# The MLP's up projection: two of its three products per chunk put side by side in one product of 512 columns

## The chip, the cores and the metric

The kernel runs on one core of a Trainium2 chip. The metric is device time in microseconds (us), the median of three runs. A core has TensorE (matrix products into the accumulator memory, PSUM), VectorE, ScalarE, GpSimd and SyncE, each with its own queue of instructions that it works off in order. They wait for each other by semaphores only.

## The reference, cut to what matters

Two transformer blocks follow each other on 256 tokens with 1024 features. The change lies in the MLP of the second block, a squared-ReLU MLP with 4096 hidden features, in float32:

```
h2 = rmsnorm(x, norm_mlp_g[l])
x = x + jnp.square(jax.nn.relu(h2 @ w_mlp_up[l])) @ w_mlp_down[l]
```

## The kernel before, in words

Float32 accuracy comes from products of a shorter type (fp32r). A number is split into a high part and a low part, and `W*X` becomes three products: high weights by high rows, high weights by low rows, low weights by high rows. `WH` and `WL` hold the two parts of the weights, in four buffers (`NB`) of 128x1024 each; one such buffer is a "unit". `XH` and `XL` hold the two parts of the rows, `HH` and `HL` those of the hidden features, both of the latter in two buffers.

The MLP is 64 units in groups of four: two up units (`k % 4` is 0 or 1) and two down units (2 or 3), so there are 16 groups. In the texts below they are called up 0, up 1, down 0 and down 1 of a group.

- An up unit (function `up` of TensorE) makes 128 hidden features of all 256 tokens. It runs over eight chunks of 128 input features, with three products of 256 columns each (`triple`, lines 1819 to 1821), all summed in the first 256 columns of bank 0 (up 0) or bank 1 (up 1). The weights are the stationary operand, the rows stream.
- VectorE then takes the ReLU out of the bank (line 1769) and squares it (line 1771), ScalarE rounds the square to its high part (line 1055), and VectorE subtracts that to have the low part (line 1774, `HL`).
- A down unit (`token_unit`, lines 2025 to 2027) multiplies the hidden features with 1024 columns of weights: 12 products of 512 columns, in which the weights stream. It waits for `relu_low`, the semaphore of line 1774: down 0 for the features of up 0, down 1 for those of up 1.

Beside that each unit has to be split: ScalarE copies it to its high part (`high2`, line 638, released by `unit_used`, which TensorE gives at the end of a unit, so that a buffer is free), and VectorE subtracts it from the weights (`low2`, line 1113, released by `unit_high`). TensorE waits for it by `unit_split`.

The order of the work is the order of the code. For a step k VectorE does `low2` of the unit three steps ahead, and then, if k is an up unit, the ReLU, the square and the low part of k's features. ScalarE does `high2` of the unit three steps ahead and then the high part of k's features. So on VectorE the ReLU of up 1 stands behind the split of the next group's up 0, and on ScalarE that split stands behind the rounding of up 0's features.

Of the kernel before, what the change touches and what calls it, by code (L numbers as in the profile page):

```python
# [8 lines left out]
F32R = mybir.dt.float32r  # L9
BF16 = mybir.dt.bfloat16  # L10
I32 = mybir.dt.int32
ALU = mybir.AluOpType
# [4 lines left out]
P = 128  # L17
D = 1024
DC = D // P
S = 256  # L20
META = 16
T = S + META
# [97 lines left out]
def build(nc, A, out):  # L120

    ctx = ExitStack()
    with ctx:
        def sb(name, shape, dt=F32):
            return ctx.enter_context(nc.sbuf_tensor(name, shape, dt))
# [5 lines left out]
        def const(name):  # L131
# [6 lines left out]
            scalar=("meta_std", "router_high", "mix_std", "group_exp", "pair_exp", "lambda_exp"),  # L138
# [18 lines left out]
        def ev(name):  # L157

            if name not in made:
                made[name] = ctx.enter_context(nc.semaphore(name))  # L160
            return made[name]
# [4 lines left out]
        big = sb("big", [P, ARENA + 8448])  # L166
        WH = sb("WH", [P, NB, UNIT], F32R)
        WL = sb("WL", [P, NB, UNIT], F32R)
        XH = sb("XH", [P, DC * T], F32R)
        XL = sb("XL", [P, DC * T], F32R)  # L170
        HH = sb("HH", [P, 2, S], F32R)
        HL = sb("HL", [P, 2, S], F32R)
        hT = sb("hT", [P, DC, T])
# [29 lines left out]
        ps = ctx.enter_context(nc.psum_tensor("ps", [P, 8, 512], F32))  # L203
# [55 lines left out]
        def z(g):  # L259
            return big[:, Z0 + g * SLAB:Z0 + (g + 1) * SLAB].rearrange("p (c t) -> p c t", c=DC)  # L260

        zx, zg, zq, zk, _, _, zc, zi = (z(g) for g in range(8))
# [33 lines left out]
        X8 = lambda t, n: t[:, 0:DC * n].rearrange("p (c t) -> p c t", c=DC)  # L296
        xh1, xl1 = X8(XH, T), X8(XL, T)
        xh2, xl2 = X8(XH, S), X8(XL, S)
        sel_part = lambda k: sel_flat[:, k * S:(k + 1) * S]
        mix_hi = [sel_part(0), sel_part(1), xh2[:, 6, :], xh2[:, 7, :], HH[:, 0, :], HH[:, 1, :], xh2[:, 2, :], xh2[:, 3, :]]  # L300
        mix_lo = [sel_part(2), sel_part(3), xl2[:, 6, :], xl2[:, 7, :], HL[:, 0, :], HL[:, 1, :], xl2[:, 2, :], xl2[:, 3, :]]
# [787 lines left out]
        def _(dve):  # L1089
            v = nc.vector  # L1090
# [16 lines left out]
            def low2(k):  # L1107
                if k >= U2:
                    return
                dve.wait_ge(ev("unit_high"), U1 + k + 1)  # L1110
                src, h = pack2(k, WH[:, k % NB, :])
                _, dst = pack2(k, WL[:, k % NB, :])
                v.tensor_tensor(dst, src, h.bitcast(F32), ALU.subtract).then_inc(ev("unit_split"), 1)  # L1113
# [62 lines left out]
            for c in range(DC):  # L1176
                dve.wait_ge(ev("x_high"), c + 1)
                v.scalar_tensor_tensor(out=xl1[:, c, :], in0=ps[:, c, 0:T], scalar=g1("pre_mix_norm", c),
                                       in1=xh1[:, c, :].bitcast(F32), op0=ALU.mult, op1=ALU.subtract)\
# [159 lines left out]
            for t in range(TT):  # L1339
# [4 lines left out]
                                       op0=ALU.mult, op1=ALU.add).then_inc(ev("mixed"), 1)  # L1344
# [5 lines left out]
                                       op0=ALU.mult, op1=ALU.add).then_inc(ev("h_mixed"), 1)  # L1350
# [4 lines left out]
            for c in range(DC):  # L1355
                dve.wait_ge(ev("turned_high"), c + 1)
                v.scalar_tensor_tensor(out=xl2[:, c, :], in0=of_chunk(c), scalar=g1("pre_ffn_norm", c),
                                       in1=xh2[:, c, :].bitcast(F32), op0=ALU.mult, op1=ALU.subtract)\
# [14 lines left out]
            for t in range(TT):  # L1373
                chain(v.scalar_tensor_tensor(out=logit[:, t, :], in0=ps[:, 3 * t, 0:nr], scalar=st(5, t),
                                             in1=b_router[:], op0=ALU.mult, op1=ALU.add))
            for t in range(TT):
                chain(v.scalar_tensor_tensor(out=logit[:, t, :], in0=ps[:, 3 * t, nr:2 * nr], scalar=st(5, t),
                                             in1=logit[:, t, :], op0=ALU.mult, op1=ALU.add))
# [19 lines left out]
            for t in range(TT):  # L1398
# [11 lines left out]
                                         op0=ALU.add, op1=ALU.mult))  # L1410
# [86 lines left out]
            for t in range(TT):  # L1497
                dve.wait_ge(ev("sh_gate"), t + 1)
                v.scalar_tensor_tensor(out=sact[:, t, :], in0=ps[:, (3, 0)[t], 0:FF], scalar=st(5, t), in1=sact[:, t, :],
                                       op0=ALU.mult, op1=ALU.mult).then_inc(ev("sh_hidden"), 1)  # L1500
# [48 lines left out]
            with dve.If(more > 0):  # L1549
                with dve.Fori(0, ROUNDS - 1) as r:  # L1550
# [4 lines left out]
                    with dve.Fori(0, QUADS) as q:  # L1555
                        b = r * QUADS + q
# [22 lines left out]
            for t in range(TT):  # L1579
# [3 lines left out]
                                             in0=ps[:, 4 + 2 * t:6 + 2 * t, :], scalar=st(8, t),  # L1583
                                             in1=gain_ffn.rearrange("p (b n) -> p b n", b=2),
                                             op0=ALU.mult, op1=ALU.mult))
                v.scalar_tensor_tensor(out=in_order(ffn_tmp[:, t, :]), in0=by_row(h_tok[:, t, :]), scalar=st(4, t),
                                       in1=in_order(ffn_tmp[:, t, :]), op0=ALU.mult, op1=ALU.add)\
# [6 lines left out]
            for c in range(DC):  # L1594
                dve.wait_ge(ev("turned_high"), DC + c + 1)
                v.scalar_tensor_tensor(out=xl2[:, c, :], in0=of_chunk(c), scalar=g2("norm_mix_g_2", c),
                                       in1=xh2[:, c, :].bitcast(F32), op0=ALU.mult, op1=ALU.subtract)\
# [11 lines left out]
            for k in range(48):  # L1609
# [4 lines left out]
                if 8 <= k < 16:  # L1614
                    c = k - 8
                    dve.wait_ge(ev("unit_taken_by_scalar"), TAKEN_S1 + c + 1)
                    w = lambda tap: g2("conv_w_2", 8 * tap + c)
                    chain(v.tensor_scalar(zc[:, c, :], zx[:, c, :], w(3), g2("conv_b_2", c), ALU.mult, ALU.add))
                    for back in (1, 2, 3):
                        ins = v.scalar_tensor_tensor(out=zc[:, c, back:], in0=zx[:, c, 0:S - back],  # L1620
                                                     scalar=w(3 - back), in1=zc[:, c, back:], op0=ALU.mult,
                                                     op1=ALU.add)
# [10 lines left out]
                if 30 <= k < 34:  # L1633
# [5 lines left out]
                                           op1=ALU.mult).then_inc(ev("one_plus_a"), 1)  # L1639
# [5 lines left out]
                if 39 <= k < 43:  # L1645
                    if k == 39:
                        dve.wait_ge(ev("lru_input"), 4)
                    for c in (2 * (k - 39), 2 * (k - 39) + 1):
                        v.tensor_tensor_scan(out=zc[:, c, :], data0=zx[:, c, :], data1=zi[:, c, :], initial=0.0,
                                             op0=ALU.mult, op1=ALU.add).then_inc(ev("scanned"), 1)  # L1650
# [15 lines left out]
            for n in range(HEADS2):  # L1666
                j, qt = divmod(n, TT)
                keys = (qt + 1) * P
                b = n % 2
# [5 lines left out]
                for h in range(2):  # L1675
                    ins = v.tensor_tensor_scan(out=cum(b)[:, h, S - keys:S][:, ::-1], data0=omb[:, h, ::-1],  # L1676
                                               data1=ones[:, 0:1].to_broadcast([P, keys]), initial=1.0,
                                               op0=ALU.mult, op1=ALU.mult)
# [83 lines left out]
            for k in range(64):  # L1762
                if k < 63:
                    low2(U_MLP + 3 + k)
                if k % 4 < 2:
                    f = (k // 4) * 2 + k % 4
                    dve.wait_ge(ev("unit_used"), U1 + U_MLP + k + 1)
                    x_ = ps[:, k % 4, 0:S]
                    v.tensor_scalar(zx[:, 2 + f % 2, :], x_, 0.0, None, ALU.max).then_inc(ev("relu"), 1)
                    dve.wait_ge(ev("relu"), f + 1)  # L1770
                    v.tensor_tensor(zx[:, f % 2, :], zx[:, 2 + f % 2, :], zx[:, 2 + f % 2, :], ALU.mult)\  # L1771
                        .then_inc(ev("relu_done"), 1)
                    dve.wait_ge(ev("relu_high"), f + 1)
                    v.tensor_tensor(HL[:, f % 2, :], zx[:, f % 2, :], HH[:, f % 2, :].bitcast(F32), ALU.subtract)\  # L1774
                        .then_inc(ev("relu_low"), 1)
                if k == 10:
                    dve.wait_ge(ev("tok_square"), 5 * TT)
                    chain(v.tensor_scalar(st(12), st(12), 1.0 / D, EPS, ALU.mult, ALU.add))
                    chain(v.reciprocal(st(13), st(12)))
# [24 lines left out]
            for t in range(TT):  # L1804
# [3 lines left out]
                                       op0=ALU.mult, op1=ALU.mult).then_inc(ev("out_tokens"), 1)  # L1808
# [5 lines left out]
        def _(pe):  # L1814
            mm = nc.tensor.matmul

            def triple(o, h, l, rh, rl, first, last, skip=False):

                mm(o, h, rh, start=first, stop=False, skip_group_check=skip)  # L1819
                mm(o, h, rl, start=False, stop=False, skip_group_check=skip)  # L1820
                return mm(o, l, rh, start=False, stop=last, skip_group_check=skip)  # L1821
# [101 lines left out]
            b = uk % NB  # L1923
            for h in range(HEADS):
                if h >= 4:
                    pe.wait_ge(ev("nope_keys_taken"), h - 3)
                w = slice(h * NOPE, h * NOPE + P)
# [6 lines left out]
            for k in range(3):  # L1934
                w = slice(HEADS * NOPE, UNIT)
# [83 lines left out]
            def used_after(last):  # L2019
                last.then_inc(ev("unit_used"), 1)  # L2020
# [8 lines left out]
            for k in range(4):  # L2029
                pe.wait_ge(ev("mix_low"), in_mix(k))  # L2030
                for t in range(TT):
                    last = mix_rows(k, t, 4)
# [8 lines left out]
            for k in range(4, 8):  # L2041
                last = mix_rows(k, 0, 0)
# [29 lines left out]
            for c in range(DC):  # L2072
# [5 lines left out]
                for t in range(TT):  # L2078
# [3 lines left out]
                    last = mm(ps[:, 3 * t, 0:nr], xl2[:, c, tk], router_hi[:, c, :], start=False, stop=c == DC - 1,  # L2082
                              skip_group_check=True)
# [112 lines left out]
            for f in range(2):  # L2196
                for t in range(TT):
                    last = tr(ps[:, 2, f * S + t * P:f * S + (t + 1) * P], sact[:, t, f * P:(f + 1) * P], ident[:])
# [16 lines left out]
            for k in range(2):  # L2215
                un = u0 + 4 + k
                pe.wait_ge(ev("unit_split"), un + 1)
                for t in range(TT):
                    tk = slice(t * P, (t + 1) * P)
                    for n in range(2):  # L2220
                        last = triple_rows(ps[:, 4 + 2 * t + n, :], HH[:, k, tk], HL[:, k, tk], un % NB, n, k == 0, False,
                                           skip=True)
# [44 lines left out]
            with pe.If(more > 0):  # L2267
                pe.wait_ge(ev("ffn_summed"), TT)
                pe.sem_inc(ev("o_by_tensor"), 1)
                with pe.Fori(0, ROUNDS - 1) as r:  # L2270
                    with pe.Fori(0, QUADS) as q:
                        b = r * QUADS + q
# [4 lines left out]
                        for t in range(TT):  # L2277
                            last = tr(ps[:, 3, t * P:(t + 1) * P], sel_w[:, t, 0:SLOTS], ident[:])
# [102 lines left out]
            for n in range(HEADS2):  # L2381
# [9 lines left out]
                for h in range(2):  # L2391
                    for k in range(nk):
                        last = tr(ps[:, (4, 7)[n % 2], (h * nk + k) * P:(h * nk + k + 1) * P],
                                  att(n % 2)[:, h, k * P:(k + 1) * P], ident[:])
# [6 lines left out]
            for c in range(2):  # L2401
                for t in range(TT):
                    last = tr(ps[:, c, t * P:(t + 1) * P], p_tok(t)[:, c * P:(c + 1) * P], ident[:])
# [27 lines left out]
            for c in range(4, DC):  # L2431
                pe.wait_ge(ev("split_low"), SP_AT["y_att"] + c + 1)
                last = token_unit(U_BRA + c, c, 0, xh2, xl2, 4, False, c == DC - 1)
# [16 lines left out]
            for c in range(4, DC):  # L2450
                last = token_unit(U_OUT + c, c, 0, xh2, xl2, 0, False, c == DC - 1)
# [13 lines left out]
            def up(k, arrived=False):  # L2465

                pe.wait_ge(ev("unit_split"), U1 + U_MLP + k + 1)
                b = (U_MLP + k) % NB
                for c in range(DC):
                    if arrived:  # L2470
                        pe.wait_ge(ev("rows_low"), 4 + 2 + c // 4 + 1)
                    w = slice(c * P, (c + 1) * P)
                    last = triple(ps[:, k % 4, 0:S], WH[:, b, w], WL[:, b, w], xh2[:, c, :], xl2[:, c, :], c == 0,
                                  c == DC - 1)
                used_after(last)

            for k in range(62):
                if k % 4 < 2:
                    up(k, k == 0)
                else:  # L2480
                    f = (k // 4) * 2 + k % 2
# [5 lines left out]
            for f in range(2):  # L2487
                pe.wait_ge(ev("relu_low"), 30 + f + 1)
                last = token_unit(U_MLP + 62 + f, f, 0, HH, HL, 4, False, f == 1)
# [14 lines left out]
            for c in range(4, DC):  # L2504
                pe.wait_ge(ev("rows_low"), 10)
                last = token_unit(U_PLE + c, c, 0, xh2, xl2, 4, False, c == DC - 1)
# [21 lines left out]
```

## Time and profile before

| | |
|---|---|
| median of three runs | 913.47 us (910.93 to 914.49) |
| the profiled execution's own time | 910.93 us |
| its span in the trace | 909.1 us |
| TensorE products, busy | 811.3 us (89%) |
| VectorE busy | 490.1 us (54%) |
| ScalarE busy | 380.0 us (42%) |
| mean TensorE clock granted | 0.956 |

The trace gives each instruction its start and its length. Ends of products are modelled, since they overlap; their starts are what counts, and the distance from one start to the next is called the pitch here. In an answer by groups, "idle before" is the time in which the engine stood still just ahead of these instructions, with the engine and line that released it. Weight loads are listed apart (PEld), since they overlap with products. The granted clock is a share of 2.4 GHz. The MLP takes the stretch from 691.6 us to some 872 us of the span.

### The profile page before, as it was taken

The page shows a single profiled execution, that of the slowest core. Times are in us where ns is not written, and L with a number is a line of the kernel's source. Part 1 is how long each engine was busy: PE and PEld are TensorE (multiplying, and loading weights), DVE is VectorE, ACT ScalarE, POOL GpSimd, SP SyncE. Part 2 cuts the span into 40 slices and gives each one's busy share as a digit, 9 for nine tenths or more (in the row PEclk, how much of TensorE's full clock was granted, in tenths as well). Part 3 has the DMA queues.
Part 4 walks back from the last instruction along what each step waited for, and adds up shares of the span by engine and source line. Part 5 has one row for each costly group of instructions (what it writes and reads, how often), then busy time and mean ns, then how long its engine had stood idle before and what let it go on. Part 6 is the DMA issues. An engine that isn't in the chain of part 4 may idle for free.

```text
span 909.1 us, 13427 instructions
## 1 busy us (share of the span) xinstructions
PE 811.3 (89%) x5498; PEld 646.6 (71%) x5498; DVE 490.1 (54%) x813; ACT 380.0 (42%) x633; POOL 48.3 (5%) x114
## 2 busy tenths in 40 slices
PE   6988999997786676779999998799999999999995
PEld 5967878764343333449989885477787999999974
DVE  6786648411110030064926687855677666666665
ACT  5563567310000100065456845535445544444454
POOL 5000030101010001000000000000000000000000
PEclk9998999999897989899999997999999999999998
DMA  8951154699999999996428552065454555555101
GB/s 278 376 188 47 48 217 177 251 411 423 422 420 420 421 421 421 413 345 212 139 70 306 193 197 81 1 240 177 161 186 144 187 187 190 189 189 195 65 1 46
DMA packets 75949, 205.80 MB, mean 226 GB/s; under 512 B 5720, under 2 KB 48896, under 8 KB 63600
## 3 DMA queue, kind: packets, MB, share of 16 engines
q1 hardware_dynamic: 67406, 150.44, 46.3%
q0 software_dynamic: 8480, 54.49, 14.9%
q8 instruction: 45, 0.74, 0.3%
q14 instruction: 16, 0.13, 0.0%
q10 hardware_dynamic: 2, 0.00, 0.0%
HBM read 203.87 MB, written 1.05 MB: 225 GB/s over the span
## 4 chain that ended last, share of the span: by engine, by line
PE 67%; DMA 16%; DVE 10%; ACT 4%; issue 2%; SPq 0%; POOL 0%; ACTq 0%; DVEq 0%
DMA big<-in_w_up 13%; PE ps L2025 10%; PE ps L2026 10%; PE ps L2027 10%; PE ps L1819 8%; PE ps L1821 7%; PE ps L1820 7%; PE ps L2138 4%; DMA big<-in_w_down 3%; PE ps L2119 1%; DVE big L1676 1%; PE ps L2152 1%; DVE WL L1105 1%; DVE WL L1113 1%; ACT WH L638 1%
## 5 line engine op out<-in xcount | busy, mean ns | idle before, releaser
L1113 DVE TENSOR_TENSOR WL<-big,WH 128x1024 fp32r<-128x1024 f32 x154 | 186.8, 1224 | 117.6 <-ACT WH L638 116.7
L638 ACT ACTIVATE WH<-big 128x1024 fp32r<-128x1024 f32 x154 | 160.6, 1054 | 83.0 <-PE ps L2027 82.5
L1819 PE MATMUL ps<-XH,WH 128*128 128x256 f32 (+1 forms) x640 | 187.4, 293 | 1.7 <-DVE WL L1105 0.7
L1820 PE MATMUL ps<-XL,WH 128*128 128x256 f32 (+1 forms) x640 | 183.1, 286 | 0.0
L1821 PE MATMUL ps<-XH,WL 128*128 128x256 f32 (+1 forms) x640 | 183.0, 286 | 0.0
L1819 PEld LDWEIGHTS ps<-XH,WH 128*128 128x128 f32 x640 | 123.6, 193 | 7.3 <-issue 4.4
L1820 PEld LDWEIGHTS ps<-XL,WH 128*128 128x128 f32 x640 | 123.8, 193 | 0.8
L1821 PEld LDWEIGHTS ps<-XH,WL 128*128 128x128 f32 x640 | 123.5, 193 | 0.0
L2138 PE MATMUL ps<-big 128*32 128x256 f32 x1024 | 75.7, 461 | 44.1 <-DMA big<-in_w_gate 26.4
L2138 PEld LDWEIGHTS ps<-big 128*32 128x32 f32 x1024 | 42.3, 132 | 78.7 <-issue 67.7
L2025 PE MATMUL ps<-WH,XH 128*128 128x512 f32 x240 | 94.4, 393 | 2.9 <-issue 1.1
L2027 PE MATMUL ps<-WL,XH 128*128 128x512 f32 x240 | 93.5, 390 | 0.0
L2026 PE MATMUL ps<-WH,XL 128*128 128x512 f32 x240 | 93.5, 389 | 0.0
L1481 DVE TENSOR_TENSOR big<-big,ps 128x256 f32<-128x256 f32 x8 | 3.4, 422 | 124.9 <-ACT big L873 124.8
L2025 PE MATMUL ps<-WH,HH 128*128 128x512 f32 x152 | 59.9, 394 | 0.6 <-DVE HL L1774 0.6
L2026 PE MATMUL ps<-WH,HL 128*128 128x512 f32 x152 | 59.4, 391 | 0.0
L2027 PE MATMUL ps<-WL,HH 128*128 128x512 f32 x152 | 59.2, 390 | 0.0
L2025 PEld LDWEIGHTS ps<-WH,XH 128*128 128x128 f32 x240 | 45.1, 188 | 13.6 <-issue 1.5
L1105 DVE TENSOR_TENSOR WL<-big,WH 128x1024 fp32r<-128x1024 f32 (+1 forms) x39 | 40.4, 1045 | 26.1 <-ACT WH L629 25.9
L2027 PEld LDWEIGHTS ps<-WL,XH 128*128 128x128 f32 x240 | 45.1, 188 | 9.6
L2026 PEld LDWEIGHTS ps<-WH,XL 128*128 128x128 f32 x240 | 45.1, 188 | 9.0
L1055 ACT ACTIVATE HH<-big 128x256 fp32r<-128x256 f32 x32 | 13.4, 418 | 76.1 <-DVE big L1771 76.1
(396 smaller groups left out, 1096.6 us busy)
## 6 DMA issues: line engine op xcount, KB each, us to landing
big<-in_w_in SPq DMA_DIRECT2D x35, 1024.0 KB, 9.5
big<-in_w_gate SPq DMA_DIRECT2D x16, 1024.0 KB, 15.6
big<-in_w_up SPq DMA_DIRECT2D x16, 1024.0 KB, 15.7
big<-in_w_gate POOLq DMA_DIRECT2D x16, 1024.0 KB, 18.8
big<-in_w_up POOLq DMA_DIRECT2D x16, 1024.0 KB, 19.4
big<-in_w_down SPq DMA_DIRECT2D x16, 1024.0 KB, 16.1
big<-in_w_down POOLq DMA_DIRECT2D x16, 1024.0 KB, 19.4
big<-in_w_mlp_up SPq DMA_DIRECT2D x16, 1024.0 KB, 5.5
```

Of the source, the lines that this page charges most:

```text
L638: s.activation(dst, src, ACT.Copy).then_inc(ev("unit_high"), 1)
L1055: s.activation(HH[:, f % 2, :], zx[:, f % 2, :], ACT.Copy).then_inc(ev("relu_high"), 1)
L1105: v.tensor_tensor(dst, src, h.bitcast(F32), ALU.subtract).then_inc(ev("unit_split"), 1)
L1113: v.tensor_tensor(dst, src, h.bitcast(F32), ALU.subtract).then_inc(ev("unit_split"), 1)
L1676: ins = v.tensor_tensor_scan(out=cum(b)[:, h, S - keys:S][:, ::-1], data0=omb[:, h, ::-1], data1=ones[:, 0:1].to_broadcast([P, keys]), ini ...
L1819: mm(o, h, rh, start=first, stop=False, skip_group_check=skip)
L1820: mm(o, h, rl, start=False, stop=False, skip_group_check=skip)
L1821: return mm(o, l, rh, start=False, stop=last, skip_group_check=skip)
L2025: mm(o, h, WH[:, b, w], start=first, stop=False, skip_group_check=skip)
L2026: mm(o, l, WH[:, b, w], start=False, stop=False, skip_group_check=skip)
L2027: return mm(o, h, WL[:, b, w], start=False, stop=last, skip_group_check=skip)
L2138: last = mm(ps[j * CAP:(j + 1) * CAP, 1, up * FF:(up + 1) * FF], x(c)[:, j * CAP:(j + 1) * CAP], slot(first_slot + j)[:, c * FF:(c + 1) * FF],
```

## The change

The high and low parts of the rows become two planes of one tensor, `XHL`, so that one product can read 256 columns of each. Per chunk, `up` now issues one product of 512 columns (high weights by high rows and by low rows, into the two halves of a bank) and one of 256 columns (low weights by high rows, into the first half). The bank's halves are then to be added: VectorE copies the first half out, adds the second, and takes ReLU and square in one instruction. The rest of the kernel is as it was, but for line numbers (1113 becomes 1114, 1774 becomes 1777, 2025 to 2027 become 2028 to 2030).

```diff
-        XH = sb("XH", [P, DC * T], F32R)
-        XL = sb("XL", [P, DC * T], F32R)
+        XHL = sb("XHL", [P, 2, DC * T], F32R)
+        XH, XL = XHL[:, 0], XHL[:, 1]
...
+        both2 = lambda c: XHL[:, :, c * S:(c + 1) * S]
...
                     dve.wait_ge(ev("unit_used"), U1 + U_MLP + k + 1)
-                    x_ = ps[:, k % 4, 0:S]
-                    v.tensor_scalar(zx[:, 2 + f % 2, :], x_, 0.0, None, ALU.max).then_inc(ev("relu"), 1)
+                    chain(v.tensor_copy(zx[:, 2 + f % 2, :], ps[:, k % 4, 0:S]))
+                    v.tensor_tensor(zx[:, 2 + f % 2, :], zx[:, 2 + f % 2, :], ps[:, k % 4, S:2 * S], ALU.add)\
+                        .then_inc(ev("relu"), 1)
                     dve.wait_ge(ev("relu"), f + 1)
-                    v.tensor_tensor(zx[:, f % 2, :], zx[:, 2 + f % 2, :], zx[:, 2 + f % 2, :], ALU.mult)\
+                    v.scalar_tensor_tensor(out=zx[:, f % 2, :], in0=zx[:, 2 + f % 2, :], scalar=0.0,
+                                           in1=zx[:, 2 + f % 2, :], op0=ALU.max, op1=ALU.mult)\
                         .then_inc(ev("relu_done"), 1)
...
-                    last = triple(ps[:, k % 4, 0:S], WH[:, b, w], WL[:, b, w], xh2[:, c, :], xl2[:, c, :], c == 0,
-                                  c == DC - 1)
+                    mm(ps[:, k % 4, :].rearrange("p (h n) -> p h n", h=2), WH[:, b, w], both2(c), start=c == 0, stop=False)
+                    last = mm(ps[:, k % 4, 0:S], WL[:, b, w], xh2[:, c, :], start=False, stop=c == DC - 1)
```

On VectorE, a stretch of the MLP before, from the low part of up 1's features on (L1113 is `low2`; `HL` the low part of the hidden features):

```order
L1774 TENSOR_TENSOR HL<-big,HH 128x256 [waits relu_high]
L1113 TENSOR_TENSOR WL<-big,WH 128x1024 [waits unit_high] x3
L1769 TENSOR_SCALAR big<-ps 128x256 [waits unit_used]
L1771 TENSOR_TENSOR big<-big 128x256 [waits relu]
L1774 TENSOR_TENSOR HL<-big,HH 128x256 [waits relu_high]
L1113 TENSOR_TENSOR WL<-big,WH 128x1024 [waits unit_high]
L1769 TENSOR_SCALAR big<-ps 128x256 [waits unit_used]
L1771 TENSOR_TENSOR big<-big 128x256 [waits relu]
L1774 TENSOR_TENSOR HL<-big,HH 128x256 [waits relu_high]
```

And the same stretch now:

```order
L1777 TENSOR_TENSOR HL<-big,HH 128x256 [waits relu_high]
L1114 TENSOR_TENSOR WL<-big,WH 128x1024 [waits unit_high] x3
L1769 COPY big<-ps 128x256 [waits unit_used]
L1770 TENSOR_TENSOR big<-big,ps 128x256 [waits vector_step]
L1773 SCALAR_TENSOR_TENSOR big<-big 128x256 [waits relu]
L1777 TENSOR_TENSOR HL<-big,HH 128x256 [waits relu_high]
L1114 TENSOR_TENSOR WL<-big,WH 128x1024 [waits unit_high]
L1769 COPY big<-ps 128x256 [waits unit_used]
L1770 TENSOR_TENSOR big<-big,ps 128x256 [waits vector_step]
L1773 SCALAR_TENSOR_TENSOR big<-big 128x256 [waits relu]
L1777 TENSOR_TENSOR HL<-big,HH 128x256 [waits relu_high]
```

Two instructions per up unit have become three, each waiting for the one ahead of it; where the split of weights stands among them has not moved. On TensorE, the start of an up unit before:

```order
L1819 MATMUL ps<-XH,WH 128x256 [waits unit_split]
L1820 MATMUL ps<-XL,WH 128x256
L1821 MATMUL ps<-XH,WL 128x256
L1819 MATMUL ps<-XH,WH 128x256
L1820 MATMUL ps<-XL,WH 128x256
L1821 MATMUL ps<-XH,WL 128x256
```

And now:

```order
L2476 MATMUL ps<-XHL,WH 128x512 [waits unit_split]
L2477 MATMUL ps<-XHL,WL 128x256
L2476 MATMUL ps<-XHL,WH 128x512
L2477 MATMUL ps<-XHL,WL 128x256
```

24 products of an up unit have become 16, for the same 6144 columns; no product has changed its place.

## Rows read from the trace of the kernel before

**Rows 1.** Busy time by engine in the MLP; PE, PEld, DVE, ACT, POOL, clock, DMA.
```profile
698.00:869.00 171.00, 170.60 (x1089) 154.60 (x1088) 111.49 (x155) 73.60 (x97) 0.00 (x0) 1.00 0.51 166
```

**Rows 2.** Groups of instructions by line, from 698 to 869 us: idle before them last.
```profile
L1819 PE MATMUL ps<-XH,WH 128*128 128x256 f32 x240 | 67.8, 283 | 0.0
L2025 PE MATMUL ps<-WH,HH 128*128 128x512 f32 x123 | 48.3, 393 | 0.6 <-DVE HL L1774 0.6
```

**Rows 3.** Timeline of one group of four units: start, length, engine, line; all engines.
```profile
760.14 0.28 PE L1819 MATMUL ps<-XH,WH 128*128 128x256 f32 x1
...
762.90 0.28 PE L1821 MATMUL ps<-XH,WL 128*128 128x256 f32 x1
...
763.22 0.42 DVE L1769 TENSOR_SCALAR big<-ps 128x256 f32<-128x256 f32 x1 [0.56 <-PE ps L1821]
...
763.68 0.42 DVE L1771 TENSOR_TENSOR big<-big 128x256 f32<-128x256 f32 x1
...
764.14 0.42 ACT L1055 ACTIVATE HH<-big 128x256 fp32r<-128x256 f32 x1 [2.73 <-DVE big L1771]
...
764.46 1.04 ACT L638 ACTIVATE WH<-big 128x1024 fp32r<-128x1024 f32 x1
...
764.59 0.42 DVE L1774 TENSOR_TENSOR HL<-big,HH 128x256 fp32r<-128x256 f32 x1 [0.48 <-ACT HH L1055]
...
765.53 1.23 DVE L1113 TENSOR_TENSOR WL<-big,WH 128x1024 fp32r<-128x1024 f32 x1 [0.52 <-ACT WH L638]
...
765.90 0.40 PE L2025 MATMUL ps<-WH,HH 128*128 128x512 f32 x1
...
766.67 0.42 DVE L1769 TENSOR_SCALAR big<-ps 128x256 f32<-128x256 f32 x1
...
768.03 0.42 DVE L1774 TENSOR_TENSOR HL<-big,HH 128x256 fp32r<-128x256 f32 x1 [0.48 <-ACT HH L1055]
...
768.42 0.39 PE L2027 MATMUL ps<-WL,HH 128*128 128x512 f32 x1
768.51 0.19 PEld L2025 LDWEIGHTS ps<-WH,HH 128*128 128x128 f32 x1
768.64 0.39 PE L2025 MATMUL ps<-WH,HH 128*128 128x512 f32 x1
...
771.37 0.28 PE L1819 MATMUL ps<-XH,WH 128*128 128x256 f32 x1
```

**Rows 4.** Timeline of VectorE in the first group of the MLP.
```profile
700.64 0.43 DVE L1774 TENSOR_TENSOR HL<-big,HH 128x256 fp32r<-128x256 f32 x1 [0.48 <-ACT HH L1055]
```

**Rows 5.** Timeline of TensorE there, at the start of down 1.
```profile
701.12 0.50 PE L2025 MATMUL ps<-WH,HH 128*128 128x512 f32 x1 [0.40 <-DVE HL L1774]
701.46 0.40 PE L2026 MATMUL ps<-WH,HL 128*128 128x512 f32 x1
```

**Rows 6.** Groups of VectorE by line and shape, whole span.
```profile
L1262 DVE SCALAR_TENSOR_TENSOR big<-big,vec 128x256 f32<-128x256 f32 x8 | 3.9, 484 | 0.3
...
L1486 DVE COPY big<-ps 128x256 f32<-128x256 f32 x8 | 3.4, 423 | 16.7 <-PE ps L2145 16.7
L1481 DVE TENSOR_TENSOR big<-big,ps 128x256 f32<-128x256 f32 x8 | 3.4, 422 | 124.9 <-ACT big L873 124.8
...
L1638 DVE SCALAR_TENSOR_TENSOR big<-big 128x512 f32<-128x512 f32 x4 | 2.7, 685 | 0.0
L1644 DVE TENSOR_TENSOR big<-big 128x512 f32<-128x512 f32 x4 | 2.7, 684 | 0.0
...
L1260 DVE TENSOR_SCALAR big<-big,vec 128x256 f32<-128x256 f32 x4 | 1.4, 353 | 0.1
```

**Rows 7.** Busy time by engine around an idle stretch of TensorE; columns as in rows 1.
```profile
397.00:398.00 1.00, 0.00 (x0) 0.00 (x0) 1.00 (x1) 0.25 (x1) 0.00 (x0) 1.00 1.09 357
400.00:401.00 1.00, 1.00 (x3) 0.71 (x3) 0.96 (x2) 1.00 (x2) 0.00 (x0) 0.50 1.11 350
```

**Rows 8.** The same, ten us in which TensorE stands still for one.
```profile
630.00:640.00 10.00, 8.93 (x40) 7.09 (x39) 6.10 (x12) 5.64 (x11) 0.00 (x0) 1.00 0.49 194
```

## The prediction

> **What bounds the kernel now.** I read first the busy time by engine in the MLP. TensorE is busy for 170.60 of 171 us at the full clock, 2.4 GHz, and VectorE for 111.49 [rows 1]. The groups by line agree: the products of the up units have no idle time before them, those of the down units 0.6 us in all, released by the low part of the hidden features [rows 2]. So TensorE seems to be the only bound, and a change that saves it time seems a gain. The reader should not stop there: a busy engine doesn't tell how near the next bound is. For that I read the timeline of one group of four units, from the first product of up 0 at 760.14 to that of the next group at 771.37, 11.23 us [rows 3], and in it the way from the end of up 0 to the start of down 1, step by step:
>
> - last product of up 0 starts 762.90; VectorE's ReLU starts at 763.22, the square at 763.68, ScalarE's rounding at 764.14;
> - ScalarE starts the split of the next up 0 at 764.46. It could have started when up 0 ended, but stands behind the rounding. VectorE's part of that split starts at 765.53;
> - VectorE's ReLU of up 1 starts at 766.67 though up 1 ended near 766.0: it stands behind the split. Its low part starts at 768.03;
> - the first weight load of down 1 starts at 768.51, its product at 768.64.
>
> No step waits for anything else, so from 762.90 to 768.51 it is one chain of 5.61 us. The load stands 0.09 us behind the product at 768.42, where loads otherwise start with the product ahead of them, and 768.03 + 0.48 = 768.51. That this is the moment of release, and no chance, the first group tells, where TensorE truly waits: low part at 700.64, product at 701.12, again 0.48 later, with 0.40 us idle put down to it [rows 4, 5]. And there the product after it comes 0.34 us later, where it otherwise takes 0.23: a waiting start costs 0.11 more. So in the group of rows 3 a waiting start would have been worth a product at 768.51 + 0.11 = 768.62; the real one is at 768.64. The slack of this chain is 0.02 us. TensorE and the chain of VectorE and ScalarE are equally long.
>
> **What the change saves on TensorE.** 24 products of 256 columns take (762.90 - 760.14) / 23 = 0.120 us each; the 12 products of 512 columns of down 1 take (771.37 - 768.64) / 12 = 0.2275 each [rows 3]. Two short ones are 0.240, one long is 0.2275, so a chunk saves 0.0125, a unit of eight chunks 0.10, and the 32 up units 3.2 us. All 768 columns of a chunk are still streamed; only the fixed time of one product goes.
>
> The Trainium skill, in VectorE: DVE Perf Modes, section on the TRN2 errata, gives a product 6 cycles of 2.4 GHz on top of its columns, 2.5 ns. By that a unit would save 0.02 us and not 0.10; the rows say 13 ns and I go by them. The sum below would be 14.0 by the page.
>
> What no row shows is a product that reads its moving columns from two planes. Lower bound of its pitch: the columns alone, 768 / 2.4 GHz = 0.320 us a chunk, which saves 0.32 a unit. Upper bound: each such product pays the 0.11 of a waiting start, 0.88 a unit. I take the pitch of the other 512-column products, the nearest row.
>
> **What it adds on VectorE.** Per up unit ReLU and square (two instructions) become copy, addition, ReLU with square (three). The copy out of PSUM is 0.423, an addition with one operand in PSUM 0.422; with an immediate scalar the fused form at 512 columns takes 685 ns where a plain product of two tensors takes 684, so at 256 it should take what the square takes, 0.42 [rows 6]. So nothing gets shorter and one instruction more is in the line. Its pitch is that from ReLU to square, 763.22 to 763.68 with the rounding again 0.46 later [rows 3]: 0.455. Bounds: the fused form could cost 0.484, as with a vector as scalar (+0.06 a unit); a copy could cost 0.353, as an operation out of SBUF does (-0.07 a unit) [rows 6].
>
> That last one is what the Trainium skill allows and forbids: VectorE: DVE Perf Modes, section Why PSUM operands drop a tier, has float32 run at the single rate whenever an operand is in PSUM. The row of the copy, 423 against 353, agrees; without that rule the sum would be 2.2 us less.
>
> **Beside or on the path.** VectorE has room as a whole (111.49 of 171), but the new instructions lie on the chain: once in up 0's part (they delay the rounding, thus ScalarE's split, thus VectorE's split), once in up 1's. The chain grows by 2 x 0.455 = 0.91, from 5.61 to 6.52, and down 1 then always begins with a waiting start, +0.11. From the last product of up 0 to the effective start of down 1: before 5.74, now 6.63. Behind the late instructions stand on VectorE the splits of the next up 1 and down 0. The first of them starts 0.95 after the low part that down 1 waits for (0.52 of it the wait for ScalarE after the 0.42) and is done before down 1 ends; TensorE wants it a whole up unit after that: no cost. Down 0 wants the low part of up 0. With up 0 ending 0.10 earlier that is there at 762.80 + 0.32 + 4 x 0.455 + 0.48 = 765.42; down 0, at 765.90 in rows 3, would now start at 765.70 by the savings of two units, and 0.11 ahead of that, at 765.59, its load has to be free. It fits by 0.17 us.
>
> Of TensorE's savings only those of up 0 count, since the chain begins at its end. Those of up 1 are added to the wait. A group becomes (2.76 - 0.10) + 6.63 + 2.73 = 12.02 us, +0.79. For 15 groups that is 11.85. The first group waits already, for both its down units, with its ReLU behind the split and not behind up 0: +0.91. Sum: +12.8 us. On the profiled execution's own time, 910.93, that gives 923.7. That execution is the fastest of the three; their median is 2.54 higher, and on it the same sum gives 926.3. I say 926.
>
> **Rivals.**
>
> 1. TensorE stays the bound: the savings come out and the additions are hidden. For it: TensorE 99.8% busy, VectorE 65% [rows 1], and hardly a wait in rows 2. Against: the timing of the weight load in rows 3 against rows 4 and 5. It decides if the real slack of the chain is above 0.91 us per group instead of 0.02. Then 32 x 0.10 = 3.2 us are gained: 913.47 - 3.2 = 910.3. This is the side of "not slower".
> 2. Reading two planes is slow. At 0.11 per product, up 0 takes 0.88 more than I say, and up 1's growth still fits under the wait (0.12 + 2.78 + 0.88 + 2.73 = 6.51 against 6.63): 16 x 0.88 = 14.1 on top, 940. Against: the bytes per column are the same.
> 3. The products profit more than by the fixed time of one: at 0.320 a chunk, up 0 saves 0.32 instead of 0.10, 16 x 0.22 = 3.5 less than my forecast, 922.5. Even the columns alone don't pay for the chain.
> 4. The clock falls, because TensorE now stands still once per group. After a stretch with no product at all, of which one microsecond is shown, TensorE was granted half the clock, 1.2 GHz [rows 7]; with 1.07 us of ten idle it kept the full clock [rows 8], and this is nearer to what the change makes, 0.9 of 12. At 1.2 GHz the 11.03 us of a group's products take 22.06, so each group that falls costs 10 us: one gives 936. The Trainium skill, in TensorE: Matmul & The Clock Gate, section A second HAM failure mode, says that short idles between groups of products can make the clock swing; rows 8 speak against it at this density.
> 5. The change not doing what it says: the order shows 16 products of the announced sizes per unit, so I give it nothing.
>
> **How the numbers follow.** Forecast 0.86, in itself 923.5 to 928.5 (the 2.2 us less of a fast copy, the 0.06 x 32 = 1.9 more of a slow fused form). Rival 1 0.05, rival 2 0.03, rival 3 0.03, rival 4 0.03. The range is 920 to 931: it takes in rival 3 and both bounds of VectorE's instructions, and some drift of the median, since three runs of the kernel before differ by 3.6 us. What a measurement of this kernel can tell from no change is about 0.5%, 4.6 us: rival 1 gains 0.35% and so counts as the same. Faster 0.02, same 0.05, slower 0.93.
>
> **What would show it.** In the changed profile: the pitch from one 512-column up product over its 256-column one to the next 512 is 0.347 us; a group lasts 12.0 us; TensorE's products have some 0.7 us of idle time before down 1 in all 16 groups, released by the low part of the hidden features (line 1777), and comes 0.48 after its start; copy, addition and fused ReLU follow each other at 0.455; down 0 has no idle before it but in the first group; the clock stays at 1.00. The chain that ended last leads through VectorE and ScalarE all along the MLP. The prediction is wrong if down 1 starts without idle time, if the up products' pitch is not near 0.347, or if down 0 begins to wait too, since its margin is only 0.17 us.

## The result, and the profile after

The changed kernel takes 925.88 us (median of five runs, 924.27 to 926.46), the kernel before 914.49 (910.93 to 915.62) in the same five rounds. The ratio is 1.0135, 95% interval 1.0107 to 1.0163: slower, by some 12 us. The forecast was 926, in a range of 920 to 931.

The profiled execution has a span of 922.5 us, 13.4 more than before. First the MLP by engine, in the columns of [rows 1]:

```profile
698.00:883.00 185.00, 174.01 (x853) 141.76 (x851) 125.00 (x187) 74.16 (x97) 0.00 (x0) 1.00 0.47 152
```

TensorE is no longer busy all the time: 11 of 185 us are idle. The granted clock is still 1.00. The groups by line, from 698 to 880 us, say what released it; these lines answer to [rows 2]:

```profile
L2476 PE MATMUL ps<-XHL,WH 128*128 128x512 f32 x240 | 85.3, 398 | 0.0
...
L2477 PE MATMUL ps<-XHL,WL 128*128 128x256 f32 x240 | 67.4, 281 | 0.0
...
L2028 PE MATMUL ps<-WH,HH 128*128 128x512 f32 x121 | 49.3, 407 | 11.1 <-DVE HL L1777 11.1
...
L1777 DVE TENSOR_TENSOR HL<-big,HH 128x256 fp32r<-128x256 f32 x30 | 12.8, 426 | 14.5 <-ACT HH L1056 14.5
L1773 DVE SCALAR_TENSOR_TENSOR big<-big 128x256 f32<-128x256 f32 x30 | 12.8, 426 | 1.0
L1769 DVE COPY big<-ps 128x256 f32<-128x256 f32 x30 | 12.6, 421 | 7.1 <-PE ps L2477 7.1
L1770 DVE TENSOR_TENSOR big<-big,ps 128x256 f32<-128x256 f32 x30 | 12.6, 421 | 1.0
```

The wait went from 0.6 to 11.1 us, all of it before the down units and put down to the low part of the hidden features. The three VectorE instructions cost 421, 421 and 426 ns, where [rows 6] had let expect 423, 422 and about 420. The timeline of one group, as in [rows 3]:

```profile
752.82 0.39 PE L2476 MATMUL ps<-XHL,WH 128*128 128x512 f32 x1
...
755.51 0.28 PE L2477 MATMUL ps<-XHL,WL 128*128 128x256 f32 x1
...
755.83 0.42 DVE L1769 COPY big<-ps 128x256 f32<-128x256 f32 x1 [0.49 <-PE ps L2477]
...
756.29 0.42 DVE L1770 TENSOR_TENSOR big<-big,ps 128x256 f32<-128x256 f32 x1
...
756.75 0.43 DVE L1773 SCALAR_TENSOR_TENSOR big<-big 128x256 f32<-128x256 f32 x1
...
757.21 0.42 ACT L1056 ACTIVATE HH<-big 128x256 fp32r<-128x256 f32 x1 [3.12 <-DVE big L1773]
...
757.53 1.04 ACT L639 ACTIVATE WH<-big 128x1024 fp32r<-128x1024 f32 x1
...
758.46 0.40 PE L2028 MATMUL ps<-WH,HH 128*128 128x512 f32 x1
...
758.61 1.23 DVE L1114 TENSOR_TENSOR WL<-big,WH 128x1024 fp32r<-128x1024 f32 x1 [0.52 <-ACT WH L639]
...
759.75 0.42 DVE L1769 COPY big<-ps 128x256 f32<-128x256 f32 x1
...
761.57 0.43 DVE L1777 TENSOR_TENSOR HL<-big,HH 128x256 fp32r<-128x256 f32 x1 [0.48 <-ACT HH L1056]
...
762.05 0.50 PE L2028 MATMUL ps<-WH,HH 128*128 128x512 f32 x1 [0.68 <-DVE HL L1777]
...
762.38 0.39 PE L2029 MATMUL ps<-WH,HL 128*128 128x512 f32 x1
...
764.91 0.39 PE L2476 MATMUL ps<-XHL,WH 128*128 128x512 f32 x1
```

The chain can be followed step by step: up 0 ends (755.51), three instructions of VectorE 0.46 apart, rounding, ScalarE's split of the next up 0 behind it (757.53), VectorE's part of that split (758.61), and only then up 1's features (759.75) and down 1 (762.05). Down 0 starts at 758.46 without idle time. The group lasts 12.09 us, before 11.23.

The chain of work that ended last, as a share of the whole span by engine, has moved the same way. First the kernel before, then the changed one:

```profile
PE 67%; DMA 16%; DVE 10%; ACT 4%; issue 2%; SPq 0%; POOL 0%; ACTq 0%; DVEq 0%
```

```profile
PE 58%; DMA 16%; DVE 16%; ACT 6%; issue 3%; SPq 0%; POOL 0%; ACTq 0%; DVEq 0%
```

In the group of [rows 3] this chain was made of TensorE's products alone. In the group above it goes through every instruction of VectorE and ScalarE just named.

### The profile page after: what moved, and what is told of

Read it like the earlier page. It is cut to its first block, busy times and chain, and to the rows that moved or that the text cites. A ratio compares the mean times of both kernels' runs of the same rounds, so it can differ in the third digit from the quotient of the medians.

```text
span 922.5 us, 12947 instructions
## 1 busy us (share of the span) xinstructions
PE 810.6 (88%) x5242; PEld 630.2 (68%) x5242; DVE 503.8 (55%) x845; ACT 380.0 (41%) x633; POOL 48.4 (5%) x114
## 4 chain that ended last, share of the span: by engine, by line
PE 58%; DMA 16%; DVE 16%; ACT 6%; issue 3%; SPq 0%; POOL 0%; ACTq 0%; DVEq 0%
PE ps L2028 9%; PE ps L2030 8%; PE ps L2029 8%; DMA big<-in_w_down 8%; DMA big<-in_w_up 7%; PE ps L1822 5%; PE ps L1824 4%; PE ps L1823 4%; PE ps L2141 3%; PE ps L2476 3%; DVE WL L1114 3%; ACT WH L639 2%; PE ps L2155 2%; DVE big L1677 2%; PE ps L2477 2%
## 5 line engine op out<-in xcount | busy, mean ns | idle before, releaser
L1822 PE MATMUL ps<-XHL,WH 128*128 128x256 f32 (+1 forms) x384 | 114.2, 297 | 1.5 <-DVE WL L1106 0.7
L1824 PE MATMUL ps<-XHL,WL 128*128 128x256 f32 (+1 forms) x384 | 109.9, 286 | 0.0
L1823 PE MATMUL ps<-XHL,WH 128*128 128x256 f32 (+1 forms) x384 | 109.9, 286 | 0.0
L2028 PE MATMUL ps<-WH,XHL 128*128 128x512 f32 x240 | 94.4, 393 | 2.9 <-issue 1.1
L2030 PE MATMUL ps<-WL,XHL 128*128 128x512 f32 x240 | 93.5, 390 | 0.0
L2029 PE MATMUL ps<-WH,XHL 128*128 128x512 f32 x240 | 93.4, 389 | 0.0
L2476 PE MATMUL ps<-XHL,WH 128*128 128x512 f32 x256 | 91.0, 398 | 0.0
L1822 PEld LDWEIGHTS ps<-XHL,WH 128*128 128x128 f32 x384 | 73.8, 192 | 6.2 <-issue 3.6
L1823 PEld LDWEIGHTS ps<-XHL,WH 128*128 128x128 f32 x384 | 73.9, 192 | 0.1
L1824 PEld LDWEIGHTS ps<-XHL,WL 128*128 128x128 f32 x384 | 73.7, 192 | 0.0
L2028 PE MATMUL ps<-WH,HH 128*128 128x512 f32 x152 | 61.8, 406 | 11.7 <-DVE HL L1777 11.7
L2477 PE MATMUL ps<-XHL,WL 128*128 128x256 f32 x256 | 71.8, 281 | 0.0
L2476 PEld LDWEIGHTS ps<-XHL,WH 128*128 128x128 f32 x256 | 48.1, 188 | 11.8
L2028 PEld LDWEIGHTS ps<-WH,XHL 128*128 128x128 f32 x240 | 45.1, 188 | 13.6 <-issue 1.5
```

What stands on the lines that cost most here:

```text
L2028: mm(o, h, WH[:, b, w], start=first, stop=False, skip_group_check=skip)
L2029: mm(o, l, WH[:, b, w], start=False, stop=False, skip_group_check=skip)
L2030: return mm(o, h, WL[:, b, w], start=False, stop=last, skip_group_check=skip)
L2476: mm(ps[:, k % 4, :].rearrange("p (h n) -> p h n", h=2), WH[:, b, w], both2(c), start=c == 0, stop=False)
L2477: last = mm(ps[:, k % 4, 0:S], WL[:, b, w], xh2[:, c, :], start=False, stop=c == DC - 1)
```

## The experiments

The total time scatters by several us from run to run, because what comes before the MLP does: in the profiles the first up product starts between 691.1 and 695.7 us, whatever the kernel, and what follows the MLP takes 36.2 to 36.3 us in all of them. So beside the ratio each experiment is read by two numbers of its profile that this doesn't touch: how long a group lasts (first up product to first up product, mean of groups 2 to 15), and the MLP's length, from the first up product to the first turning (transposing, on TensorE) of its result. Each ratio is to the kernel before as it ran in the same session. The diffs show each edit against the changed kernel, but for VectorE's part alone, whose edit is against the kernel before; "..." marks lines left out.

| kernel | ratio to before (95%) | group, us | first group | MLP, us |
|---|---|---|---|---|
| before | 1 | 11.23 | 12.44 | 181.25 |
| the change | 1.0135 (1.0107 to 1.0163) | 12.10 | 13.35 | 195.13 |
| TensorE's part alone | 0.9993 (0.9969 to 1.0016) | 11.18 | 12.41 | 180.50 |
| VectorE's part alone | 1.0148 (1.0119 to 1.0177) | 12.16 | 13.33 | 196.03 |
| change, up 1's features first | 0.9976 (0.9953 to 0.9999) | 11.11 | 12.14 | 179.44 |
| before, up 1's features first | 0.9986 (0.9970 to 1.0002) | 11.22 | 11.66 | 180.34 |
| change, copy twice | 1.0340 (1.0308 to 1.0372) | 13.00 | 14.25 | 209.61 |
| change, copy twice in up 0 | 1.0246 (1.0199 to 1.0293) | 12.54 | 13.81 | 202.33 |
| change, one stretch | 1.0170 (1.0140 to 1.0200) | 12.09 | 13.35 | 194.99 |
| change, both first | 0.9992 (0.9966 to 1.0018) | 11.11 | 11.47 | 178.76 |
| before, both first | 0.9982 (0.9961 to 1.0003) | 11.22 | 11.22 | 179.89 |
| change, both products long | one run, 938.35 us | 12.93 | 13.31 | 207.54 |

**TensorE's part alone.**

```diff
-                    chain(v.tensor_copy(zx[:, 2 + f % 2, :], ps[:, k % 4, 0:S]))
-                    v.tensor_tensor(zx[:, 2 + f % 2, :], zx[:, 2 + f % 2, :], ps[:, k % 4, S:2 * S], ALU.add)\
-                        .then_inc(ev("relu"), 1)
+                    x_ = ps[:, k % 4, 0:S]
+                    v.tensor_scalar(zx[:, 2 + f % 2, :], x_, 0.0, None, ALU.max).then_inc(ev("relu"), 1)
...
-                    v.scalar_tensor_tensor(out=zx[:, f % 2, :], in0=zx[:, 2 + f % 2, :], scalar=0.0,
-                                           in1=zx[:, 2 + f % 2, :], op0=ALU.max, op1=ALU.mult)\
+                    v.tensor_tensor(zx[:, f % 2, :], zx[:, 2 + f % 2, :], zx[:, 2 + f % 2, :], ALU.mult)\
```

> TensorE's part of the change alone: the product of 512 columns stays, VectorE takes ReLU and square of the first half only, with the two instructions of the kernel before. The result lacks the products of high weights by low rows. Changed profile: the pitch of a pair of products is 0.353 us, so an up unit saves 0.06. Theory (the chain from the end of up 0 to down 1 is as long as TensorE's work, slack 0.02): only up 0's saving counts, down 1 begins with a waiting start; a group lasts 2.70 + 5.72 + 2.73 = 11.15 us against 11.23, some 1.2 us less in all, with weight loads of down 1 released by the low part in each group. Rival (TensorE is the only bound): a group lasts 11.11 us, 1.9 us less in all, and no load of down 1 waits more than before.

A group lasts 11.18 us, 0.05 less; the MLP is 0.75 shorter. The product of 512 columns brings little even with nothing added, and the waits say why. First the kernel before, then this one, from 698 to 869 us (who waited for whom: us in total, times, longest):

```profile
PEld ps L2025 <- DVE HL L1774: 0.8, 1, 0.8
```

```profile
PEld ps L2026 <- DVE HL L1775: 4.1, 16, 0.9
```

One load was held before and 16 are now, so the chain is already the longer of the two. The rival had 11.11 us and no new waits; it falls. The gain of 0.05 is smaller than the 0.08 of the theory. In the group that starts at 786.37 the part up to the end of up 0 (2.69) and the chain with its waiting start (5.73) are as expected to 0.01, but down 1 takes 2.77 in place of 2.73; why its products come a little slower after a wait is open. The total can't tell any of this from no change.

**VectorE's part alone.**

```diff
+                    chain(v.tensor_copy(zx[:, 2 + f % 2, :], ps[:, k % 4, 0:S]))
                     x_ = ps[:, k % 4, 0:S]
```

> VectorE's part alone: the products of the kernel before, and one copy out of PSUM ahead of the ReLU in every up unit, so three instructions in place of two. Theory: the chain grows by 2 x 0.455 us, a group lasts 12.12 us (+0.89), all in all +14.3 us, about 0.9 more than the whole change, ratio to before 1.0156. Rival (the loss comes from the two-plane products or from the clock): the ratio stays within 0.2% of 1.

The ratio is 1.0148, a group takes 12.16 us, the MLP is 14.8 us longer, 0.9 more than in the whole change, as expected. With the products of the kernel before, the whole loss is there, and the rival falls. The cost of the change is this one instruction more per up unit.

**The change with up 1's features first.**

```diff
-                if k < 63:
+                if k < 63 and not (k % 4 == 1):
                     low2(U_MLP + 3 + k)
...
                         .then_inc(ev("relu_low"), 1)
+                if k % 4 == 1:
+                    low2(U_MLP + 3 + k)
```

> The whole change, with one step of VectorE's order moved: for up 1 the copy, addition, square and low part of the features come ahead of the split of the next group's up 0. Theory: that takes ScalarE's and VectorE's split out of the chain; from the last product of up 1 to the release of down 1 are 0.32 + 4 x 0.455 + 0.48 = 2.62 us, needed within 2.74. So down 1 waits no more, a group lasts 2 x 2.82 + 2 x 2.73 = 11.10 us, and in all some 2.1 us less than before: ratio 0.9977. Rival (VectorE's total work or the additions in themselves are the cost): a group stays near 12 us, ratio near 1.013.

The same instructions on every engine, one of them per group in another place, and the loss is gone: a group lasts 11.11 us, and the MLP is 1.8 us shorter than before. On VectorE's timeline:

```profile
766.34 0.42 DVE L1769 COPY big<-ps 128x256 f32<-128x256 f32 x1 [0.49 <-PE ps L2479]
...
768.16 0.43 DVE L1777 TENSOR_TENSOR HL<-big,HH 128x256 fp32r<-128x256 f32 x1 [0.48 <-ACT HH L1056]
769.17 0.42 DVE L1769 COPY big<-ps 128x256 f32<-128x256 f32 x1 [0.59 <-PE ps L2479]
...
770.99 0.42 DVE L1777 TENSOR_TENSOR HL<-big,HH 128x256 fp32r<-128x256 f32 x1 [0.48 <-ACT HH L1056]
771.34 3.49 DVE L1114 TENSOR_TENSOR WL<-big,WH 128x1024 fp32r<-128x1024 f32 x3
```

Up 1's copy now waits for TensorE (0.59 us idle) and not for a split, and the three splits come in a row behind. So neither VectorE's total work nor the addition in itself was the cost; its place in the chain was.

**The kernel before with the same order** (the same edit).

> The kernel before with the same move on VectorE (up 1's features ahead of the next split). Theory: TensorE is as long as the chain was, so a group stays at 11.21 to 11.23 us, and only the first group, in which down 1 waited, gains some 0.7 us: ratio 0.999. Rival (the chain costs the kernel before time in every group): more than 2 us less.

A group lasts 11.22 us against a mean of 11.23, and the first group is 0.78 shorter. Here all groups after the first take 11.22; in the kernel before, four of the fourteen take 11.25 or 11.26. So there the chain cost TensorE only 0.01 us per group on the mean: the two were equally long, as it had been read off [rows 3 to 5]. It takes both, the product of 512 columns and the new order, to gain 0.11 per group.

**The copy twice, in both up units and in up 0 alone.**

```diff
                     chain(v.tensor_copy(zx[:, 2 + f % 2, :], ps[:, k % 4, 0:S]))
+                    chain(v.tensor_copy(zx[:, 2 + f % 2, :], ps[:, k % 4, 0:S]))
```

> The whole change with the copy out of PSUM done twice in both up units of a group. Theory: every VectorE instruction ahead of the square lies in the chain once per up unit, so another 2 x 0.455 us per group: a group lasts 12.10 + 0.91 = 13.0 us, some 14.6 us on top of the change, ratio to before about 1.030. Rival (the chain has room and the loss is elsewhere): under 3 us on top.

```diff
                     chain(v.tensor_copy(zx[:, 2 + f % 2, :], ps[:, k % 4, 0:S]))
+                    if k % 4 == 0:
+                        chain(v.tensor_copy(zx[:, 2 + f % 2, :], ps[:, k % 4, 0:S]))
```

> The same second copy, but only in up 0. Theory: up 0's instruction delays down 1 as much as up 1's does, though down 1 does not read up 0's features, because ScalarE's split of the next up 0 stands behind the rounding of up 0's features and VectorE's split behind that. So half of the experiment with both: a group lasts 12.55 us, +7.3 us on top of the change. Down 0 begins to wait too (its margin of 0.17 us is gone), which costs nothing more since down 1 waits anyhow. Rival (only up 1's instructions matter for down 1): under 1 us on top.

Groups of 13.00 and 12.54 us; the MLP grows by 14.5 and 7.2 us over the change, where 14.6 and 7.3 were expected. The second shows what is least visible in the code: down 1 doesn't read up 0's features, and yet an instruction in up 0's part delays it by its full 0.45. VectorE in that kernel:

```profile
762.64 0.43 DVE L1779 TENSOR_TENSOR HL<-big,HH 128x256 fp32r<-128x256 f32 x1 [0.48 <-ACT HH L1056]
763.59 1.23 DVE L1114 TENSOR_TENSOR WL<-big,WH 128x1024 fp32r<-128x1024 f32 x1 [0.52 <-ACT WH L639]
764.73 0.41 DVE L1769 COPY big<-ps 128x256 f32<-128x256 f32 x1
...
766.54 0.43 DVE L1779 TENSOR_TENSOR HL<-big,HH 128x256 fp32r<-128x256 f32 x1 [0.48 <-ACT HH L1056]
```

Then TensorE's weight load at the start of down 0, and its first product of down 1:

```profile
763.12 0.19 PEld L2030 LDWEIGHTS ps<-WH,HH 128*128 128x128 f32 x1 [0.29 <-DVE HL L1779]
...
767.02 0.50 PE L2030 MATMUL ps<-WH,HH 128*128 128x512 f32 x1 [0.89 <-DVE HL L1779]
```

VectorE's split waits for ScalarE behind up 0's low part, and up 1's copy for that split. The release again comes 0.48 after the low part's start. Down 0's load is now held as well, by 0.29 us, and as expected this costs nothing more. The ratios, 1.034 and 1.025, are above the expected 1.030 and the 1.022 that +7.3 us gives. The 1.022 lies inside its interval, the 1.030 just below it (1.0308). The same excess shows in the next experiment, which ran beside these two: its MLP is that of the changed kernel to within 0.2 us, and yet its ratio is 1.0170 where the change had 1.0135. So it lies outside the MLP; whether it is more than scatter isn't shown.

**One stretch in place of two planes.**

```diff
-both2(c), start=c == 0
+XH[:, (c // 2) * 2 * S:(c // 2) * 2 * S + 2 * S].rearrange("p (h n) -> p h n", h=2), start=c == 0
```

> The whole change, but the product of 512 columns reads one contiguous stretch of the high rows (two neighbouring chunks) in place of two planes. The result is that of other rows: it multiplies the high weights by the high rows of a wrong chunk in place of the low rows. If reading from two planes is what makes the pair's pitch 0.353 us where 0.2275 + 0.120 = 0.3475 was forecast, the pair here takes 0.3475 and a group 0.04 us less. Rival (a long and a short product in turn cost 0.005 us more whatever they read): the pitch stays 0.353.

The pitch is that of the changed kernel, as the rival had it: the long products start at 754.95, 755.29, 755.64, 756.00, 756.35 and 756.70, 0.35 apart. The 32 products of up 0 and up 1 take 5.64 us here and in the changed kernel. Two planes cost nothing.

**Both products long.**

```diff
-                    last = mm(ps[:, k % 4, 0:S], WL[:, b, w], xh2[:, c, :], start=False, stop=c == DC - 1)
+                    last = mm(ps[:, k % 4, :].rearrange("p (h n) -> p h n", h=2), WL[:, b, w], both2(c), start=False, stop=c == DC - 1)
```

> The whole change, with the second product of each pair also reading both planes (low weights by high and low rows, 512 columns), so 256 columns more per chunk, which adds the product of low weights by low rows. It measures the pitch of a long product in the up units by itself. If a long product here takes 0.2275 us as in the down units, a pair takes 0.455, and the 0.005 us more per pair of the changed kernel come from long and short taking turns. If it takes 0.233 or more, a pair takes 0.466 or more and the up unit's long product is itself slower than the down unit's. Time is only a side matter here: about 0.85 us more per up 0, while up 1's growth goes into the wait of down 1: some 13 us more than the changed kernel.

TensorE's timeline, the first up product of the MLP, the last one and what follows:

```profile
692.73 0.39 PE L2476 MATMUL ps<-XHL,WH 128*128 128x512 f32 x1
...
699.75 0.39 PE L2477 MATMUL ps<-XHL,WL 128*128 128x512 f32 x1
699.98 0.39 PE L2028 MATMUL ps<-WH,HH 128*128 128x512 f32 x1
```

32 products in 7.25 us (692.73 to 699.98) are 0.2266 each. So a long one among long ones takes what it takes in the down units (0.2275), a short one among short ones 0.120, and a pair in turn 0.353 in place of 0.347: taking turns costs 0.006. Why is open.

**Both first**, in the change and in the kernel before: the condition of the third experiment becomes `k == 0 or k % 4 == 1`.

> The whole change with features ahead of the split for up 1 of every group and also for up 0 of the first group. Expected beside the version with up 1 alone: in the first group down 0 starts without waiting for the split, some 0.5 us less; other groups as there, 11.10 us. In all 2.7 us less than before, ratio 0.997. Rival: no difference that can be measured to the version with up 1 alone.

> The kernel before with features ahead of the split for up 1 of every group and for up 0 of the first. Expected: groups of 11.22 us as with up 1 alone, down 0 of the first group without its wait; from the first up product to the turning of the MLP's result some 179.8 us, against 181.25 in the kernel before and 178.8 in the changed kernel with the same order. If so, the product of 512 columns itself is worth about 1.0 to 1.8 us once the order lets it, and the order alone 1.5. Ratio to before 0.998.

In the change the first group now lasts 11.47 us and the MLP 178.76; in the kernel before they last 11.22 and 179.89. The product of 512 columns is worth 1.1 us of 180 once the chain is out of its way: 0.11 in each of the 15 groups after the first, 1.65 in all, less what is lost in the first group (0.25) and where the MLP's result is turned (TensorE is idle for 0.53 us there, against 0.21). By the whole time the two can't be told from each other, nor from the kernel before. The change with up 1's features first is ahead of the kernel before by 0.24%, with an interval that just leaves out 1; its MLP, 1.8 us or 0.2% of the whole time shorter, agrees. No version here beats the kernel before by more than about that.

## Why the prediction was right

- **The bound.** It rested on one reading: a weight load 0.09 us behind its product's predecessor, taken as a release and not as chance, hence a slack of 0.02 us. It was shown right from three sides. Shortening TensorE's part held 16 loads in place of one; lengthening the chain by 0.91 us made a group 0.93 longer; and taking the split out of the chain gave the kernel before only 0.01 us per group.
- **TensorE's saving, mis-sized.** The forecast added two pitches of unmixed streams, 0.347 us a pair. Up 0 of the group shown takes 755.51 - 752.82 + 0.12 = 2.81 us, 0.351 a pair, and in the first 16 pairs of the MLP it is 0.353. A unit saves 0.06 and not 0.10. In proportion this is the term that was most off.
- **VectorE's addition.** Two pitches of 0.455 were put on the chain. The chain went from 5.61 to 762.05 - 755.51 = 6.54 us, +0.93 for 0.91. The three durations came within 6 ns of what the rows had let expect; the bound of 0.484 wasn't needed.
- **The waiting start.** 762.05 to 762.38 is 0.33 where products that don't wait are 0.23 apart: 0.10 for 0.11.
- **The group.** 12.02 forecast, 12.10 measured: 0.03 from up 0, 0.02 from the chain and 0.03 from down 1, which lasts 764.91 - 762.15 = 2.76 in place of 2.73. Over 15 groups 13.0 us in place of 11.85; the first group +0.91 as forecast (13.35 against 12.44). TensorE stands still before down 1 in all 16 groups, for 0.85 us in the first and some 0.68 in the others, as announced.
- **The sum.** 12.8 forecast; the MLP grew by 13.9, the span by 13.4, since this execution came to the MLP 0.5 us earlier. By the medians it is 11.4, by the ratio 12.3. That 926 met 925.88 is partly luck. The sum was 1.1 us too small, and the base it was added to, the median of three runs (913.47), is 1.0 below the median of five that the result is set against (914.49); on that base it would have said 927.3. Single runs of one kernel differ by several us.
- **Down 0** was said to fit by 0.17 us. It has no idle time before it (758.46), and as announced the first group alone is an exception.
- **Rivals.** TensorE as the only bound (910.3): fell with the result, and its account of the waits with the first experiment. Slow planes: fell with the one stretch. More profit than a product's fixed time: the profit was smaller. The clock: it was granted at 1.00 from 698 to 883 us, with TensorE idle once per group for 0.68 us. The Trainium skill (TensorE: Matmul & The Clock Gate, A second HAM failure mode) has a kernel in which short idles between groups of products made the clock swing; this trace shows no swing.
- **The copy out of PSUM** took 421 ns, against 353 for an operation out of SBUF [rows 6]. The Trainium skill (VectorE: DVE Perf Modes, Why PSUM operands drop a tier) has float32 at the single rate when an operand is in PSUM, and the trace agrees.

## What to carry to other kernels

An engine that is busy for 99.8% can have a second chain just as long beside it. Here the busy times didn't tell, and the moment at which one weight load was released did. Before work is moved from the busiest engine to one with room, follow the way from the end of its unit to the next instruction that waits for it, through every queue that works in order; in this kernel an instruction there cost its full pitch, also where the unit that waits doesn't read its result. And the loss was mended by order alone: one split behind the features in place of ahead of them.

## What the runs showed of the hardware

- In this kernel a product of 512 columns and one of 256 in turn took 0.353 us a pair, though streams of each alone took 0.2266 and 0.120 us a product. Reading from two planes or from one stretch made no difference.
- A product that waited started 0.48 us after the start of the VectorE instruction of 256 columns that released it, in three kernels (701.12 - 700.64, 762.05 - 761.57, 767.02 - 766.54). The product behind it came 0.33 to 0.34 us later, where 0.23 is usual: a waiting start cost 0.10 to 0.11 us.
